# Further rounds of an expert: an inner loop around the unit instead of separate bodies

## The reference, cut to what matters

```
g_star = argmax(g_logits)                       # one of 4 groups
top_val, top_idx = top_k(e_logits[g_star], 2)   # two of its 8 experts
gate = p_group * softmax(top_val)
y[token] += gate * ((silu(xb @ w1[e]) * (xb @ w3[e])) @ w2[e])
x = layer_norm(alpha * x + y)
```

## Time and profile before

| | |
|---|---|
| median of 3 runs | 1472.35 us (1469.18 to 1473.29) |
| the profiled execution | 1477.09 us, its span 1475.3 us |
| PE busy | 1172.6 us, 79% of the span |
| PEld busy | 732.6 us, 50% |
| DVE busy | 397.8 us, 27% |
| ACT busy | 169.3 us, 11% |
| HBM read | 471.52 MB |

### The profile page before, as it was taken

One profiled execution on the slowest core, in us unless ns is written; L12 is line 12 of the kernel. 1 busy time (PEld: TensorE's weight loads), 2 busy tenths in 40 slices (PEclk: granted clock), 3 DMA queues, 4 the chain that ended last, 5 costly groups with the idle time before them and its releaser, 6 DMA issues.

```text
span 1475.3 us, 32893 instructions
## 1 busy us (share of the span) xinstructions
PE 1172.6 (79%) x11774; PEld 732.6 (50%) x11775; DVE 397.8 (27%) x1045; ACT 169.3 (11%) x473; POOL 30.9 (2%) x79
## 2 busy tenths in 40 slices
PE   8999999988668777668789999987887756675664
PEld 7884547554335444334458857554553333333332
DVE  1953531342112221112242131351222111111113
ACT  0211501111001010001020001110110000000001
POOL 3000000000000000000000000000000000000000
PEclk9999999999889898889889999998998888888887
DMA  9755135279999999999992465254899999999994
GB/s 312 249 189 210 58 139 203 84 281 429 426 427 428 430 427 429 429 428 428 430 397 105 171 228 213 101 201 174 343 427 427 429 430 427 430 429 427 428 429 180
DMA packets 64538, 473.25 MB, mean 321 GB/s; under 512 B 4156, under 2 KB 11644, under 8 KB 39916
## 3 DMA queue, kind: packets, MB, share of 16 engines
q1 hardware_dynamic: 62284, 465.78, 77.1%
q0 software_dynamic: 2208, 6.81, 1.3%
HBM read 471.52 MB, written 1.05 MB: 320 GB/s over the span
## 4 chain that ended last, share of the span: by engine, by line
PE 52%; DMA 36%; issue 5%; DVE 3%; ACT 1%; SPq 0%; DVEq 0%; ACTq 0%; POOL 0%; POOLq 0%
DMA ring<-in_moe_w_dram 36%; PE bank L528 14%; PE bank L925 13%; PE bank L541 8%; PE bank L941 3%; PE bank L721 2%; PE bank L949 2%; PE bank L911 2%; PE bank L501 1%; PE bank L843 1%; PE bank L932 1%; PE bank L868 1%; DVE xT L1046 1%; PE bank L825 1%; PE bank L597 0%
## 5 line engine op out<-in xcount | busy, mean ns | idle before, releaser
L925 PE MATMUL bank<-ring,xT 128*32 128x256 f32 x4672 | 358.2, 474 | 250.3 <-DMA ring<-in_moe_w_dram 190.2
L925 PEld LDWEIGHTS bank<-ring,xT 128*32 128x32 f32 x4672 | 197.9, 135 | 410.3 <-issue 303.7
L528 PE MATMUL bank<-xT,ring 128*128 128x256 f32 x832 | 183.0, 382 | 6.1 <-DVE xT L1046 4.8
L528 PEld LDWEIGHTS bank<-xT,ring 128*128 128x128 f32 x832 | 159.0, 192 | 29.2 <-issue 7.7
L1461 DVE SCALAR_TENSOR_TENSOR xT<-xT,bank 64x256 f32<-64x256 f32 x73 | 30.3, 414 | 413.1 <-ACT xT L1699 413.1
L941 PE MATMUL bank<-slot,xT 128*32 128x256 f32 x2336 | 139.6, 379 | 1.3 <-DVE xT L1471 1.3
L541 PE MATMUL bank<-ring,slot 128*128 128x512 f32 x256 | 111.5, 594 | 4.0 <-ACT slot L1677 2.0
L941 PEld LDWEIGHTS bank<-slot,xT 128*32 128x32 f32 x2336 | 78.4, 110 | 50.0 <-issue 5.9
L1699 ACT ACTIVATE xT<-bank 64x256 f32<-64x256 f32 x73 | 27.5, 377 | 587.9 <-PE bank L925 587.9
L1447 DVE TENSOR_TENSOR xT<-iota,place 128x64 f32 (+1 forms) x73 | 16.5, 225 | 276.7 <-issue 274.2
L949 PE MATMUL bank<-xT 32*128 32x256 f32 x1200 | 86.0, 400 | 4.5 <-issue 4.5
(11 more groups left out here) (271 smaller groups left out, 752.7 us busy)
## 6 DMA issues: line engine op xcount, KB each, us to landing
ring<-in_moe_w_dram SPq DMA_DIRECT2D x128, 2048.0 KB, 32.6
slot<-in_moe_w_dram SPq DMA_DIRECT2D x64, 2048.0 KB, 38.1
ring<-in_od_w_in_dram SPq DMA_DIRECT2D x6, 2048.0 KB, 20.1
ring<-in_xa_wq_dram SPq DMA_DIRECT2D x4, 2048.0 KB, 11.6
ring<-in_xa_wo_dram SPq DMA_DIRECT2D x4, 2048.0 KB, 11.5
ring<-in_ev_w_in_dram SPq DMA_DIRECT2D x3, 2048.0 KB, 14.6
ring<-in_mem_wk_dram SPq DMA_DIRECT2D x2, 2048.0 KB, 15.1
ring<-in_mem_wv_dram SPq DMA_DIRECT2D x2, 2048.0 KB, 10.7
```

The costliest lines, as they stand in the source:

```text
L528: ins = mm(ps, w[:, k, c0:c0 + P], rhs[:, k, :], start=(k == 4), stop=(k == 3))
L925: ins = mm(b1[qs[2 * m + h], 0:S], xg[:, k, :], ws[m][:, k, h, :, :], start=(k == 0), stop=(k == KC - 1))
```

## The change

The first round and the further ones are now the same code. Around each of the three units stands an inner loop of up to eight turns; behind the unit it is left when fewer than two rounds remain of `m - r`. The three separate bodies behind the loop and the branch over them are gone.

```
-                spills = []
                 with nc.Fori(0, TURNS, engines=[pe.engine], head_slot={pe.engine: 0}) as i:
                     for j in range(SETS):
                         m, first = load_units(pe, L, i * SETS + j)
                         s_ = moe_slots[L][j]
                         ready = [(i + (moe_base[L][s_[k]] + 1)) * 16 for k in range(3)]
-                        rounds = pe.to_reg(m)
+
+                        def rounds():
+
+                            before = nc.cur_bb
+                            with pe.Fori(0, ROUNDS) as r:
+                                unit(s_, ready, first + r + 1)
+                                pe.br_lt(pe.to_reg(m - r), 2, on_true=f"moe{L}_next{j}", on_false=f"moe{L}_again{j}")
+                                nc.switch_bb(f"moe{L}_again{j}")
+                            pe.br(f"moe{L}_next{j}")
+                            nc.switch_bb(f"moe{L}_next{j}", parent=before)
+
                         if j < NE % SETS:
-                            unit(s_, ready, first + 1)
+                            rounds()
                         else:
                             with pe.If(m > 0):
-                                unit(s_, ready, first + 1)
+                                rounds()
                             pe.nop()
-                        spills.append((s_, m, first, ready, nc.cur_bb))
-                        pe.br_lt(rounds, 2, on_true=f"moe{L}_next{j}", on_false=f"moe{L}_more{j}")
-                        nc.switch_bb(f"moe{L}_next{j}")
...
-                pe.br(f"moe{L}_done")
-
-
-                for j in range(SETS):
-                    s_, m, first, ready, before = spills[j]
-                    with nc.body(f"moe{L}_more{j}", parent=before, valid_engines=[pe.engine]):
-                        with pe.Fori(0, 2) as ra:
...
-                        pe.br(f"moe{L}_next{j}")
-                nc.switch_bb(f"moe{L}_done")
```

## The result

The changed kernel takes 1462.32 us (median of 10 runs, 1459.17 to 1464.66), the kernel before 1474.71 us in its 10 (1467.14 to 1483.57): 12.4 us less, a ratio of 0.991 (95% interval 0.989 to 0.993). The forecast was -16.1 us, 1456.3 us with a range of 1451 to 1463. The median of before also moved: it was 1472.35 us over its first three runs. The profiled execution of the changed kernel took 1463.68 us, its span is 1461.9 us, 13.4 us under the span of before.

The account below looks back on a forecast made before the run. Both expert stages run at the pace of the weights' DMA stream, so its start in layer 1 counts. Terms -16.9 + 0.3 + 0.5 = -16.1 us, from 1472.35 to 1456.3 us, range 1451 to 1463.

Parts of the forecast that it names:

- rival C: Only a cold edge stalls, expert 0's second round in layer 1: 6.3 us of the gain, 1462.6 us; chance 0.06.
- (1): Entering a further round by the inner loop's back edge: no idle time taken; ends 0 and 6.38 us.
- A: Inner loop's back edge stalls like an entry into the old body: three edges, 18.8 us, so 1475 us; chance 0.08.
- B: Same three layer 1 edges, dearer stall of two blocks: 8.4 us each, 25.3 us, so 1481.5 us; chance 0.05.
- (2): Coming back after a further round: one branch forward over a few instructions, taken as the ordinary step between experts.
- (3): Layer 1 from 984.78 us to release of expert 1's slots: 53.80 us becomes 36.9, 16.9 less (17.7 to 16.1).
- (4): End of layer 0, where expert 31 waits for weights and its L925 is slow: +0.3 us, bounds -1.4 and +1.3.
- (5): Inner loop's counter, longer sums and taken branch, on the path at three places: +0.5 us, between 0 and 1.3.
- Rival D: Between experts VectorE's build holds up TensorE's gather: steps over experts 0 and 1 grow 1 us each, 1458 us; chance 0.02.

Follow-up runs that it names:

- second copy beside the first: Against the changed kernel, further rounds get their own one-loop code directly behind the first round's, inside TensorE's loop; 1468.89 us, ratio 0.996.
- one-loop bodies: Against the kernel before, the separate bodies stay but hold one loop from round 1 to m, not three nested ones; 1468.64 us, ratio 0.993.
- without placing: Outer loop's head not placed at a fetch block's start: kernel before 1472.5 us, changed kernel 1460.7 us, kernel that counts to m 1457.68 us.
- before again: The kernel before, unchanged, run and profiled once more; span 1479.3 us, layer 1's head 46.26 us.
- layer 1 only: The kernel before with the new loop in layer 1 alone, layer 0 keeping its separate bodies; 1466.05 us, ratio 0.992.
- layer 0 only: The kernel before with the new loop in layer 0 alone; 1474.6 us, ratio 1.000.
- the placed kernel that counts to m: The changed kernel with the inner loop counting to m itself, replacing the test on m - r; 1462.73 us, ratio 0.991.

## Why the prediction was right, and where it was off

The place and the mechanism were right, the gain was forecast 3.7 us too large (the other 2.4 us between 1456.3 and 1462.3 are the median of before, which moved). That 1462.32 us lies inside the range is luck in part: the forecast with its own bounds and the spread ended at 1461 us, and only rival C, which did not come, carried the range to 1463.

**What bounds the kernel.** Right. Layer 0's further rounds gave nothing that the times could show (ratio 1.000), layer 1's head gave by far the most, and behind it the rest of the span is the same 436.6 to 439.3 us in the eleven traces of the table. The stalls taken away elsewhere became waits for weights: TensorE's idle time ahead of L925 by "issue" fell from 59.8 to 21.7 us, that by the weights' DMA rose from 190.2 to 221.5 us.

**(1) Entering a round.** Right: no idle time, a back edge of 0.21 us. Rivals A, B and C fall with it. The Trainium skill's rule of two blocks, which the prediction weighed, would have made each of these back edges a fetch; they go back over a whole unit of 260 and more instructions, so it doesn't hold for TensorE's queue as it stands. The same page (the Trainium skill, Runtime: NRT & Kernel Launch, section "Instruction fetch mechanics") gives TensorE a memory of 2048 instructions. With that the runs agree: a loop of six units, at least 1560 instructions, had no fetch in its later passes (q8 moved nothing from 365 to 780 us in the kernel with the second copy beside the first).

**(2) Coming back.** Right in what was left (0.85 us), and the prediction didn't say why it stalled. The one-loop bodies and the idle q8 showed it: a chain of branches, not a fetch.

**(3) The head.** This is the term that was mis-sized, in both its halves. "Afterwards" was 36.9 us and measured 35.4 to 35.6 us: a further round behind another takes 1020.83 - 1013.21 = 7.6 us, not 8.16, whose two samples came from elsewhere in the stage. "Now" was taken as 53.80 us, one execution's value, as if it were the code's. The old code's head is 53.80, 46.26, 44.07 and 47.68 us in four traces, mean 47.95; the first was the only one in which expert 1's way in stalled. 47.95 - 35.45 = 12.5 us, and the medians differ by 12.4. The forecast's -16.1 us had 16.9 from this term; with the mean of four it would have been 47.95 - 36.9 = 11.1, and the forecast 1462.1 us. That 12.5 and 12.4 come so close is luck: four traces are few, and the measured ratio allows 9.7 to 16.1 us. Whether this part that is drawn anew in each execution also makes the kernel before spread from 1467 to 1484 us (the changed one from 1459 to 1465) is not shown; without placing, the old bodies, with the same kind of stalls, spread only from 1469.7 to 1474.5 in ten runs. The first trace itself held the warning: L994 branches to a separate body eight times there, and five of these branches took 0.21 to 0.22 us.

**(4) The end of layer 0.** From the first issue to expert 31's L925 it is 752.75 - 327.95 = 424.80 us against 426.51: -1.7, and its L925 took 3.66 us, since it had waited only 1.94 us and not 5.1. So against the first trace the bound of -1.4 us came true, and a little more, not the middle of +0.3. The first trace was the shortest of its kind here: with before's code in layer 0 this stretch is 426.5 to 429.5 us in four traces, with the new code 424.6 to 425.3 in six. By the table's column up to layer 1 layer 0 gained about 2.5 us, where 0.3 us of loss were forecast.

**(5) The loop's own cost.** Right in size: 0.85 to 1.25 us at a change of expert against 0.4 to 0.9, so about 0.4, and only one on the path.

**Rival D.** Not seen: the gather (L911) idled 1.0 us for VectorE's build before and not at all in the changed kernel, and L941 1.3 us for VectorE before and 0.0 after.

**What no step had.** Layer 0's start, +6.9 us in the profiled execution. It does not need the change: late starts (first L925 of 5.8 to 6.0 us) are in before again, one-loop bodies, layer 1 only and both traces of the changed kernel; early ones in before, layer 0 only and the placed kernel that counts to m. Whether the change makes it more frequent is open, as both traces of the changed kernel have it. It does mean that the two profiled executions were unlike at a place that the change doesn't touch, and that 18.3 us in the head showed as 13.4.

## What to carry to other kernels

A stall that a trace shows once is a sample. If it is a fetch (the instruction queue moves a packet while the branch lasts), look for the branch's other occurrences in the same trace, the ones without a stall too, and sort them by whether their code was new: here the first way into far code in a layer stalled every time and a later one in two of thirty. Price the first as sure, the others by how often they stall, and take the range from the extremes. And price a stall by what waits for its end: here eight of the eleven removed (three ways in, eight ways back) lay beside a stream of weights that was the bound anyway, of them only the last of layer 0 could show in the time, and the other three set that stream's start. Rare work is best put where its code has just run: a loop around it costs 0.2 us, a far copy 3.4 to 7.5 us of fetch where it stalls, and nested tests around it a us a level each time, which the common case pays too if they stand in its way.

## What the runs showed of the hardware

- A taken branch lasts 0.21 us on TensorE's queue when its target has lately been run or fetched, and 1.5 to 7.5 us when it has not (7512 ns in the kernel changed in layer 0 only). All 27 long ones of the fourteen traces end 2.3 to 4.2 us after a packet of the instruction queue q8 has started. The same branch can do either from one execution to the next.
- Loops of three units (from 353 to 780 us in the changed kernel) and of six (from 365 to 780 us with the second copy) run their later passes without one packet of q8.
- The branch over the padding at a loop's head takes 1.6 to 5.6 us in layer 0, by when its packet starts. The granted clock doesn't tell the late start: its mean from 300 to 312 us was 0.89 to 0.92 in four late ones (both changed ones, layer 1 only, before again), but 1.00 in a fifth (one-loop bodies), and 0.86 and 0.91 in two kernels without placing that started early. What makes the packet late is open.
- Three nested loops of two, with a test each, cost 4.5 to 5.0 us of TensorE's idle time an expert although nothing is fetched, as each end of a level is a few register operations and two taken branches.
- Behind 3.3 us of idle time and more the 64 matmuls of an L925 take 4.9 to 6.6 us instead of 3.66 in 605 of the 628 cases that the fourteen timelines show whole, and in every one behind 5 us. It is not a sharp line: 3.66 us stood behind 3.32, 3.71 and 4.06 us of idle time as well, and 5.35 us behind 2.01.
